# Every float32r product with its moving operand and its PSUM output walked from the last column to the first

## What is computed

```python
def first_block(x, ...):
    h = rmsnorm(x, norm1_g)
    z = h @ w_in                       # 1024 -> conv value/gate, q, k, v, forget logits, two gates
    ya = conformer_conv(a_val, a_gate, ...) ; ob = forgetting_attention(q, k, v, c)
    x = x + (sigmoid(g_a) * ya + sigmoid(g_b) * (ob @ w_fox_out)) @ w_out
    x = x + peer_ffn(rmsnorm(x, norm2_g), ...)     # 16384 experts, top 16 of 256 pairs, 8 heads
    return rmsnorm(x, normf_g)

def second_block(x, mem, ...):
    z = rms_norm(x, norm_mix) @ w_in   # rg_lru, gated linear attention, attention over mem, 3 gates
    x = x + (sum of 3 gated branches @ w_branch) @ w_out
    up = causal_dwconv(rms_norm(x) @ w_up) ; gate_h, val_h = split(up)
    x = x + (gelu(gate_h) * val_h) @ w_down
    return rms_norm(x, final_norm)
```

## Time and profile before

| | us |
|---|---|
| median of 2 runs (1597.41 to 1597.86) | 1597.63 |
| span of the profiled execution, first to last instruction | 1595.2 |
| TensorE matmul busy | 1583.0 (99%) |
| TensorE weight load busy | 1493.5 (94%) |
| VectorE busy | 1071.3 (67%) |
| ScalarE busy | 884.2 (55%) |
| GpSimd busy | 885.8 (56%) |

### The profile page before, as it was taken

The page is one execution under the profiler, slowest core; times in us unless marked ns, Lnnn a source line. Parts: engine busy times, 40 slices in busy tenths (PEclk is TensorE's granted clock), DMA queues, the critical chain, the costliest instruction groups (busy, mean ns, idle before and its releaser), DMA issues.

```text
span 1595.2 us, 33476 instructions
## 1 busy us (share of the span) xinstructions
PE 1583.0 (99%) x12568; PEld 1493.5 (94%) x12568; DVE 1071.3 (67%) x1867; ACT 884.2 (55%) x1251; POOL 885.8 (56%) x413
## 2 busy tenths in 40 slices
PE   9999999999999999999999999999999999999998
PEld 8999899999999999998888888889999999999998
DVE  7998643779933777778888666776937383455521
ACT  6557766454454444444444445457676654666653
POOL 8786468868886000000000244457876689888886
PEclk9999999999999999999999999999999999999999
DMA  6565346555555555555555666666543356666653
GB/s 222 171 191 154 106 132 187 186 175 190 188 184 186 171 171 171 172 169 171 179 178 166 215 190 194 195 189 185 172 148 106 109 177 185 188 190 187 191 187 119
DMA packets 86218, 277.03 MB, mean 174 GB/s; under 512 B 11233, under 2 KB 18161, under 8 KB 86129
## 3 DMA queue, kind: packets, MB, share of 16 engines
q1 hardware_dynamic: 85712, 274.76, 54.9%
q0 software_dynamic: 272, 1.05, 0.2%
q10 hardware_dynamic: 144, 0.00, 0.0%
HBM read 274.73 MB, written 1.05 MB: 173 GB/s over the span
## 4 chain that ended last, share of the span: by engine, by line
PE 93%; issue 2%; DVE 2%; POOL 1%; ACT 1%; DMA 0%; SPq 0%; DVEq 0%; ACTq 0%; POOLq 0%
PE gemm L679 36%; PE gemm L982 22%; PE gemm L684 18%; PE aux L1268 4%; PE gemm L813 3%; PE aux L962 2%; POOL w_lo L462 1%; PE gemm L700 1%; PE gemm L725 1%; PE gemm L1268 1%; PE aux L932 0%; PE gemm L799 0%; ACT w_hi L1364 0%; PE gemm L706 0%; PE gemm L742 0%
## 5 line engine op out<-in xcount | busy, mean ns | idle before, releaser
L462 POOL TENSOR_TENSOR w_lo<-raw,w_hi 128x1024 fp32r<-128x1024 f32 (+1 forms) x330 | 791.7, 2407 | 294.7 <-ACT w_hi L1364 285.6
L1364 ACT ACTIVATE w_hi<-raw 128x1024 fp32r<-128x1024 f32 (+1 forms) x492 | 515.8, 1050 | 575.5 <-PE gemm L679 324.0
L679 PE MATMUL gemm<-h_lo,w_hi 128*128 128x256 f32 x2144 | 294.3, 279 | 0.0
L679 PE MATMUL gemm<-h_hi,w_hi 128*128 128x256 f32 x2096 | 293.3, 282 | 0.4 <-ACT w_hi L1364 0.3
L684 PE MATMUL gemm<-h_hi,w_lo 128*128 128x256 f32 x2096 | 288.6, 280 | 1.4 <-POOL w_lo L462 0.9
L679 PEld LDWEIGHTS gemm<-h_lo,w_hi 128*128 128x128 f32 x2144 | 268.9, 188 | 0.3 <-issue 0.2
L679 PEld LDWEIGHTS gemm<-h_hi,w_hi 128*128 128x128 f32 x2096 | 264.0, 188 | 3.3 <-issue 1.6
L462 DVE TENSOR_TENSOR w_lo<-raw,w_hi 128x1024 fp32r<-128x1024 f32 x162 | 196.6, 1222 | 104.3 <-ACT w_hi L1364 103.7
L684 PEld LDWEIGHTS gemm<-h_hi,w_lo 128*128 128x128 f32 x2096 | 262.8, 188 | 3.5 <-POOL w_lo L462 2.2
L982 PE MATMUL gemm<-w_hi,act_parts 128*128 128x512 f32 x1008 | 250.9, 391 | 0.4 <-ACT act_parts L1565 0.4
L982 PEld LDWEIGHTS gemm<-w_hi,act_parts 128*128 128x128 f32 x1008 | 188.0, 188 | 39.0 <-issue 0.5
(11 more groups left out here) (436 smaller groups left out, 2065.6 us busy)
## 6 DMA issues: line engine op xcount, KB each, us to landing
raw<-in_w_u SPq DMA_DIRECT2D x128, 512.0 KB, 3.6
raw<-in_w_ev SPq DMA_DIRECT2D x128, 512.0 KB, 3.7
raw<-in_w_up SPq DMA_DIRECT2D x48, 512.0 KB, 4.3
raw<-in_w_gate SPq DMA_DIRECT2D x24, 512.0 KB, 3.8
raw<-in_w_down SPq DMA_DIRECT2D x24, 512.0 KB, 4.0
raw<-in_w_conv_in SPq DMA_DIRECT2D x16, 512.0 KB, 4.6
raw<-in_w_peer_q SPq DMA_DIRECT2D x16, 512.0 KB, 3.5
raw<-in_w_branch SPq DMA_DIRECT2D x24, 288.0 KB, 2.9
```

Of the source, the lines that this page charges most:

```text
L462: eng.tensor_tensor(w_lo[v][:, 0:n], raw[c.raw][v][:, 0:n], w_hi[v][:, 0:n], ALU.subtract).then_inc(lo_ready[v], 1)
L679: mm = pe.matmul(out, w[:, k, :], act_part[:, k, :], start=(n == k == 0), stop=False)
L1364: act.activation(w_hi[v][:, 0:n], raw[c.raw][v][:, 0:n], ACT.Copy).then_inc(hi_ready[v], 1)
```

## The change

A helper, `back(tile)`, gives a view of the same tile in which the columns of the last axis run from the last to the first (a step of -1). In each float32r matmul the output and the moving operand are wrapped in it. Column 255 of the moving operand is then read first and its result is written first, to column 255 of the output, so that every number lands where it did. The stationary operand is as before. The number, order, sizes, waits and signals of all instructions are as before, and so are the matmuls of other types.

```diff
+        def back(tile):
+            return tile[:, ::-1]
...
-                        mm = pe.matmul(out, w[:, k, :], act_part[:, k, :], start=(n == k == 0), stop=False)
+                        mm = pe.matmul(back(out), w[:, k, :], back(act_part[:, k, :]), start=(n == k == 0), stop=False)
...
-                    mm = pe.matmul(out, w[:, k, :], x[0][:, k, :], start=False, stop=(k == steps - 1))
+                    mm = pe.matmul(back(out), w[:, k, :], back(x[0][:, k, :]), start=False, stop=(k == steps - 1))
...
-                            mm = pe.matmul(pair(gemm[c.bank])[:, tt, :],
-                                           x[:, v * KD // 2 + k, tt * P:(tt + 1) * P], w[:, k, :],
+                            mm = pe.matmul(back(pair(gemm[c.bank])[:, tt, :]),
+                                           x[:, v * KD // 2 + k, tt * P:(tt + 1) * P], back(w[:, k, :]),
...
-                                mm = pe.matmul(gemm[2 * half + tt][:, :], a[:, c.raw, v, tt * P:(tt + 1) * P],
-                                               w[v][:, half * (D // 2):(half + 1) * (D // 2)],
+                                mm = pe.matmul(back(gemm[2 * half + tt]), a[:, c.raw, v, tt * P:(tt + 1) * P],
+                                               back(w[v][:, half * (D // 2):(half + 1) * (D // 2)]),
...
-                            mm = pe.matmul(out, w[v][:, k * P:(k + 1) * P], x[:, g * KD + k, :],
+                            mm = pe.matmul(back(out), w[v][:, k * P:(k + 1) * P], back(x[:, g * KD + k, :]),
```

More of the change, by code:

```diff
@@ L699, in high @@
                         pe.wait_ge(hi_ready[v], c.split + 1)
-                    pe.matmul(both[:, v, :], hi[v][:, k, :], x[0][:, k, :], start=(v == k == 0), stop=False,
+                    pe.matmul(back(both[:, v, :]), hi[v][:, k, :], back(x[0][:, k, :]), start=(v == k == 0), stop=False,
                               skip_group_check=True)
@@ L705, in low @@
                         pe.wait_ge(lo_ready[0], c.split + 1)
-                    return pe.matmul(both[:, 0, :], lo[:, k, :], x[0][:, k, :], start=False, stop=False,
+                    return pe.matmul(back(both[:, 0, :]), lo[:, k, :], back(x[0][:, k, :]), start=False, stop=False,
                                      skip_group_check=True)
@@ L724, in paced_product @@
                             pe.wait_ge(split, before + k // step + 1)
-                        mm = pe.matmul(both[:, v, :], hi[v][:, k, :], x[1][:, k, :], start=False,
+                        mm = pe.matmul(back(both[:, v, :]), hi[v][:, k, :], back(x[1][:, k, :]), start=False,
                                        stop=(v == 0 and k == KD - 1), skip_group_check=True)
@@ L730, in paced_product @@
                 for k in range(KD):
-                    mm = pe.matmul(both[:, 1, :], lo[:, k, :], x[0][:, k, :], start=False, stop=(k == KD - 1),
+                    mm = pe.matmul(back(both[:, 1, :]), lo[:, k, :], back(x[0][:, k, :]), start=False, stop=(k == KD - 1),
                                    skip_group_check=True)
@@ L741, in part @@
                     for k in (2 * g, 2 * g + 1):
-                        mm = pe.matmul(both[:, v, :], w[v][:, k, :], x[:, k, :], start=(begins and k == 0),
+                        mm = pe.matmul(back(both[:, v, :]), w[v][:, k, :], back(x[:, k, :]), start=(begins and k == 0),
                                        stop=(ends and k == KD - 1), skip_group_check=True)
@@ L1009, in one @@
                     def one(w, a, half, tt, ends=False):
-                        return pe.matmul(gemm[2 * half + tt][:, :], a[:, c.raw, v, tt * P:(tt + 1) * P],
-                                         w[v][:, half * (D // 2):(half + 1) * (D // 2)], start=False, stop=ends,
+                        return pe.matmul(back(gemm[2 * half + tt]), a[:, c.raw, v, tt * P:(tt + 1) * P],
+                                         back(w[v][:, half * (D // 2):(half + 1) * (D // 2)]), start=False, stop=ends,
                                          skip_group_check=True)
```

## The result

The changed kernel takes 1612.32 us (median of 2 runs, 1612.20 to 1612.43), the kernel before 1597.63: a ratio of 1.0093, 95% interval 1.0063 to 1.0122. It is slower by 14.7 us, which is clear of noise but within the 2% that were called no change.

The account below looks back on a forecast made before the run. TensorE, 99% busy, was taken to bound the kernel through its matmul pitches. The terms summed to 0 + 0 + 0 on a span of 1595.2 us, plus 2.4 us outside it: 1598 us, range 1504 to 1645 us.

Parts of the forecast that it names:

- the 2% that were called no change: Whole kernel: likeliest case, no change above 2% (32 us), at 1598 us, own range 1570 to 1629; chance 0.55.
- What bounds the kernel: TensorE, busy 99%, is one long queue of matmuls that hardly waits, so the time is a sum of pitches.
- (a) Instructions and queues: All queues: no instruction, wait or queue entry added, removed or moved; weight loads stay at 188 ns; cost 0.
- (b) Reading backwards: Moving operand read from SBUF with step -1: full rate kept, cost 0, with small placement and joint effects possible.
- The bounds for the 256-column products: Placement's 1.6 ns per matmul: +10 us if h tiles lose it, -4 us if the others gain it.
- the forecast of the profile: Likeliest-case pitches: 116 to 119 ns at 256 columns, 226 to 228 at 512; h tiles and others closer or apart.
- (c) Writing PSUM backwards: Float32 output written to PSUM with step -1: least known term, taken as 0; ceiling 222.5 ns per 256-column matmul.
- R1: Reader or writer loses ascending pairs, one column in two cycles: +1315 us, 2913 us; chance 0.13.
- R2: Joint between matmuls: every backward start jumps, 4 ns per jump, +36 us, 1634 us; chance 0.08.
- R3: Reversal removes a clash of two SBUF streams: pitches 109 and 216 ns, 1504 us; gain above 2% has chance 0.22.
- R4: Both reversals folded into a forward pattern, nothing moves: 1598 us; chance counted within the likeliest case's 0.55.

Follow-up runs that it names:

- run 9: Kernel before with only spacers changed: 16 floats added ahead of xres, spacer ahead of h gone, 24 floats behind h; ratio 1.0056 to the kernel before.
- runs 5 and 9: Run 5: kernel before without the spacer ahead of h, some expert-value chunks with reordered weight halves or 64 stationary columns; span 1608.8 us. Run 9 has its own line.

## Why the prediction was right, and what it missed

**What bounds the kernel**: right. The time followed the pitches, and nothing else moved; the sum of pitches gives 15.9 where the spans differ by 15.1 us.

**(a) Instructions and queues**, 0: right, by the same counts, waits and the 188 ns.

**(b) Reading backwards**, taken as 0: right for the rate and too small for the place. The rate stayed near one column per cycle. The bounds for the 256-column products were +10 us if the h tiles lose what their place gives and -4 us if the others gain it; measured +7.2 and -1.4. So both bounds were of the right kind; most of the loss came about and a third of the gain. The two kinds came closer (117.8 and 117.8 ns), as the forecast of the profile had it. The term that I left out is the 512-column products: I had one row of them and no second place to compare with, and gave their place no price. It is +10.1 us, two thirds of the loss, and its pitch of 233.5 ns lies outside the 226 to 228 that were forecast. That is the mis-sized term: all matmuls should have had the bound. That the whole stayed within 2% was in part luck, since no row said how much the place was worth at 512 columns.

**(c) Writing PSUM backwards**, taken as 0, with a ceiling of one column in two cycles: right, the output alone backwards gives 0.9999. The page "Advanced Engine Details and Errata" of the Trainium skill, section PSUM Cachelines, wants every two consecutive elements contiguous; the runs agree with it only if a descending pair counts as that. That page of the Trainium skill names no factor: the 2913 us of R1 were priced from the plain float32 rows. R1 is excluded.

**R2**, the joint: excluded by the other order of the halves (226.9 and 233.5 ns, unchanged), and by the 256-column products, which it had all dearer by some 3.5 ns: the h products lost 1.1 and the others gained 0.5. The 2.0 ns between the excess at 512 and at 256 columns, from which I priced it, changed with the place as well (20.2 and 11.1 ns in run 9).

**R3**, two streams out of SBUF that are in each other's way: its direction was wrong; its ground, that addresses matter, was not, though a clash itself is not shown. The pitch does depend on where the moving tile stands against the others and on what the weight load reads (64 columns instead of 128: 226.7 to 230.0 ns). Turning one stream round does not free it of this, it deals the excess out anew: +6.6, +1.1 and -0.5 ns here. Its full price, 109 ns, was seen nowhere; the lowest 256-column pitch of all runs is 113.3.

**R4**, nothing at all: excluded, since the pitches moved.

What stays open is the rule by which place and start set the pitch, and by which a stretch of work takes up one of two pitches in the same place. Shown: it is on the side of SBUF reads; it depends on the tiles' addresses at a step of 32 bytes, on the walk's start and length, on the number of stationary columns, and on something that differs between two stretches of one execution (113.3 and 117.8 ns); and no direction is dearer in every place. That the weight load and the moving stream meet in some unit of SBUF is the likeliest reading and only argued. The one rule that I formed from it gave a wrong forecast for run 9. No version that computes everything beat the kernel before: without the spacer, most f and y products and some x products have 113.3 ns (the others 117.8), but the h products then have 120.0.

## What to carry to other kernels

A kernel that is one long queue of matmuls has its time in the pitch, and the pitch of float32r products here went from 113.3 to 120.0 ns with nothing changed but the place or direction of an operand, and from 113.3 to 117.8 within one execution with nothing changed at all. Read the pitch of each stretch of each stage, and not one mean, after any change of the SBUF layout, even one that is meant for something else, and price such an effect for every kind of matmul, not only for the one in which the rows happen to show it. A layout that was tuned for one walk is tuned for that walk alone: reverse or shorten it, and the places must be looked for again, by measuring them.

## What the runs showed of the hardware that I had not expected

- Descending float32 writes of TensorE into PSUM cost nothing (ratio 0.9999, interval 0.9990 to 1.0009).
- Moving tiles by 32 bytes changed the pitch of 256-column float32r matmuls from 116.7 to 120.0 ns in one place, and from 118.3 to 113.4 in another.
- The same tiles in the same place and direction had 113.3 ns in one stretch and 117.8 in another of one execution (runs 5 and 9).
- Forward 512-column matmuls at 226.7 ns didn't get faster with 508, 504 or 496 columns when the start moved with them.
- A weight load of 64 columns and not 128 (134 ns and not 188) made the forward 512-column stream slower, 230.0 ns against 226.7.
